# Inputs laid out by the host: x, mem, context and parameters without turns on TensorE

## The reference

```python
def first_block(x, mem, positions, ...):          # per layer
    proj = x @ w_in[l]
    q, k, v, cb, cc, cu, qm, gates = jnp.split(proj, ...)
    q, k = rope(q), rope(k)                        # angles from positions
    y_attn = diff_attention(q, k, v, lam, ...)     # lam from the four lambda vectors
    y_conv = short_gated_conv(cb, cc, cu, conv_w[l])
    y_mem = memory_attention(qm, mem, w_mem_kv[l])
    g = jax.nn.sigmoid(gates)
    merged = g0 * (y_attn @ w_br_attn[l]) + g1 * (y_conv @ w_br_conv[l]) + g2 * (y_mem @ w_br_mem[l])
    x = layer_norm(ALPHA * x + merged @ w_out[l], ln1_g[l], ln1_b[l])
    f = grouped_moe(x, w_router, router_bias, w_exp_gate[l], w_exp_up[l], w_exp_down[l])
    x = layer_norm(ALPHA * x + f, ln2_g[l], ln2_b[l])
```

## Time and profile before

| | us |
|---|---|
| median of 3 runs | 2258.7 |
| lowest and highest | 2258.26, 2258.95 |
| span of the profiled execution | 2261.8 |
| PE busy | 2213.9 (98%) |
| PEld busy | 1399.4 (62%) |
| DVE busy | 1144.6 (51%) |
| ACT busy | 457.5 (20%) |

### The profile page before, as it was taken

The page is one execution under the profiler, slowest core; times in us unless marked ns, Lnnn a source line. Parts: engine busy times, 40 slices in busy tenths (PEclk is TensorE's granted clock), DMA queues, the critical chain, the costliest instruction groups (busy, mean ns, idle before and its releaser), DMA issues.

```text
span 2261.8 us, 24795 instructions
## 1 busy us (share of the span) xinstructions
PE 2213.9 (98%) x9825; PEld 1399.4 (62%) x9825; DVE 1144.6 (51%) x1926; ACT 457.5 (20%) x1046; POOL 3.1 (0%) x20
## 2 busy tenths in 40 slices
PE   8999999999999999999999999999999999999998
PEld 7755444544468765446444486788888888554453
DVE  3755775211137267763111247775556423587666
ACT  2001401211121014122111236420000102352110
POOL 0000000000000000000000000000000000000000
PEclk9999999999999999999999999999999999999999
DMA  8445934799983449435999902003222124403340
GB/s 345 149 178 218 385 141 175 285 399 426 428 358 134 164 155 422 167 149 216 392 425 428 420 33 113 1 1 112 75 75 89 52 103 180 155 10 149 140 177 19
DMA packets 38800, 454.71 MB, mean 201 GB/s; under 512 B 5288, under 2 KB 9242, under 8 KB 11034
## 3 DMA queue, kind: packets, MB, share of 16 engines
q1 hardware_dynamic: 35520, 449.85, 49.2%
q10 hardware_dynamic: 3162, 3.21, 0.4%
HBM read 452.00 MB, written 1.05 MB: 200 GB/s over the span
## 4 chain that ended last, share of the span: by engine, by line
PE 82%; DMA 8%; DVE 7%; DVEq 2%; issue 1%; ACT 1%; SPq 0%; ACTq 0%
PE banks L603 79%; DMA ring<-in_w_exp_up 7%; PE banks L1726 1%; PE banks L759 1%; DVE ring L3040 1%; DVE tiny L3250 1%; DVE tiny L2589 1%; DVE arena L2603 0%; DVE arena L3265 0%; DVE ring L2334 0%; DVE arena L2308 0%; DMA ring<-in_w_in 0%; DVE banks L2586 0%; DVEq L2309 0%; PE banks L1192 0%
## 5 line engine op out<-in xcount | busy, mean ns | idle before, releaser
L603 PE MATMUL banks<-ring,arena 128*64 128x512 f32 (+2 forms) x3302 | 960.7, 546 | 14.5 <-DMA ring<-in_w_exp_up 4.9
L603 PEld LDWEIGHTS banks<-ring,arena 128*128 128x128 f32 (+1 forms) x3302 | 449.5, 166 | 485.4 <-issue 450.7
L603 PE MATMUL banks<-arena 128*128 128x128 f32 (+7 forms) x1584 | 243.9, 344 | 3.7 <-issue 1.7
L603 PE MATMUL banks<-X,ring 128*128 128x256 f32 x1024 | 224.8, 382 | 0.8 <-DVE arena L2542 0.5
L603 PEld LDWEIGHTS banks<-X,ring 128*128 128x128 f32 x1024 | 195.8, 192 | 29.7 <-issue 2.3
L603 PEld LDWEIGHTS banks<-arena 128*128 128x128 f32 (+2 forms) x1584 | 155.3, 173 | 66.4 <-issue 34.9
L603 PE MATMUL banks<-arena,ring 128*128 128x256 f32 (+1 forms) x736 | 179.1, 399 | 0.1
L603 PEld LDWEIGHTS banks<-arena,ring 128*128 128x128 f32 x736 | 138.7, 190 | 36.8 <-issue 14.4
L2433 DVE TENSOR_TENSOR arena<-arena,banks 128x512 f32<-128x512 f32 x16 | 11.0, 687 | 281.9 <-ACT arena L1874 281.9
L603 PE MATMUL banks<-ring 128*128 128x256 f32 x616 | 137.0, 379 | 0.0
L603 PEld LDWEIGHTS banks<-ring 128*128 128x128 f32 x616 | 117.0, 190 | 16.3 <-issue 0.5
(11 more groups left out here) (369 smaller groups left out, 1923.6 us busy)
## 6 DMA issues: line engine op xcount, KB each, us to landing
ring<-in_w_in SPq DMA_DIRECT2D x38, 2048.0 KB, 11.8
ring<-in_w_exp_up SPq DMA_DIRECT2D x32, 2048.0 KB, 16.2
ring<-in_w_exp_down SPq DMA_DIRECT2D x32, 2048.0 KB, 12.3
ring<-in_w_exp_gate SPq DMA_DIRECT2D x30, 2048.0 KB, 13.5
ring<-in_w_ada SPq DMA_DIRECT2D x24, 2048.0 KB, 10.7
ring<-in_w_ffn SPq DMA_DIRECT2D x22, 2048.0 KB, 7.8
ring<-in_w_out SPq DMA_DIRECT2D x8, 2048.0 KB, 13.4
ring<-in_w_down SPq DMA_DIRECT2D x8, 1408.0 KB, 6.0
```

The source lines that it names most:

```text
L603: ins = nc.tensor.matmul(out, weights, moving, start=start, stop=stop)
```

## The change

- The host lays out x, mem and the context with features on partitions (`x_turned`, `mem_turned`, `ctx_turned`, each [128, 8, 256]), and all parameter vectors as 246 columns of one array (`columns`, [128, 246]).
- All turns of these on TensorE go, with the copies out of PSUM on DVE and ACT.
- SP issues x and the first tile in three pieces each, by feature chunks 0 to 2, 2 to 4 and 4 to 8; the matmuls of the first tile go in the same three pieces.
- SP no longer waits for the parameters ahead of the third tile. DVE, ACT and TensorE each wait for all of them (8 transfers now) where they come to need them: TensorE after the second tile.
- mem, the rows of x (for the residual sum) and the context are issued by SP after `w_br_conv`'s tile.

```diff
-PARAM_DMAS = 23
+PARAM_DMAS = 8
+FIRST_PIECES = ((0, 2), (2, 4), (4, 8))
...
-            for tc in range(TC):
-                sp.dma_start(raw["x"][:, tc, :], a["x"][tc * P:tc * P + P, :]).then_inc(s_x[tc], 16)
...
-                    if l == 0 and i == 2:
-                        sp.dma_start(raw["mem"], a["mem"].rearrange("(c p) d -> p c d", p=P)).then_inc(s_inputs, 16)
-                        sp.wait_ge(s_params, PARAM_DMAS * 16)
                     src = block_of("w_in", l * 16 + c)
                     if l == 0 and i == 0:
-                        sp.dma_start(ring[:, 0, 0:TILE // 2], src[:, 0:TILE // 2]).then_inc(s_half_tile, 16)
-                        sp.dma_start(ring[:, 0, TILE // 2:TILE], src[:, TILE // 2:TILE]).then_inc(s_loaded[0], 16)
+                        for n, (k0, k1) in enumerate(FIRST_PIECES):
+                            landed = s_tile_piece[n] if n < len(s_tile_piece) else s_loaded[0]
+                            sp.dma_start(X[:, k0:k1, 0:T], a["x_turned"][:, k0:k1, :]).then_inc(s_x[n], 16)
+                            sp.dma_start(ring[:, 0, k0 * 512:k1 * 512], src[:, k0 * 512:k1 * 512]).then_inc(landed, 16)
...
                 tile(block_of("w_br_conv", l))
                 if l == 0:
+                    sp.dma_start(memT[:], a["mem_turned"]).then_inc(s_inputs, 16)
+                    sp.dma_start(xres, a["x"].rearrange("(c p) d -> p c d", p=P)).then_inc(s_x_rows, 16)
+                    sp.dma_start(X[:, :, T:2 * T], a["ctx_turned"]).then_inc(s_ctx_loaded, 16)
...
-            pe.wait_ge(s_half_tile, 16)
-            for half in range(2):
-                pe.wait_ge(*x_copied[half])
-                if half:
+            for n, (k0, k1) in enumerate(FIRST_PIECES):
+                pe.wait_ge(s_x[n], 16)
+                if k1 < DC:
+                    pe.wait_ge(s_tile_piece[n], 16)
+                else:
                     next_tile()
                 for c, b in enumerate(FIRST_BANKS):
-                    for k in range(4 * half, 4 * half + 4):
+                    for k in range(k0, k1):
...
             tile_features(X, T, "act")
-            pe.wait_ge(s_inputs, 16)
             pe.wait_ge(s_params, PARAM_DMAS * 16)
-            b = ring_bank("dve")
-            nc.tensor.transpose(bank[b][:, 0:104], stackA[0:104, :], ident[0:104, 0:104])
...
-            turned_input("mem", "act")
...
-                    pe.wait_ge(s_ctx_loaded, 16)
-                    turned_input("ctx_2", "act", lambda k0, k1: filler(1, k0, k1))
-                    filler(1, 6, DC)
+                    filler(1, 0, DC)
...
             act.dma_start(pos_i, a["positions"][0, :].partition_broadcast(P)).then_inc(s_turns, 16)
             act.dma_start(invf[:], a["inv_freq"]).then_inc(s_turns, 16)
+            act.dma_start(vecs[:], a["columns"]).then_inc(s_params, 16)
             for i, n in enumerate(("lambda_q1", "lambda_k1", "lambda_q2", "lambda_k2")):
                 act.dma_start(lamrows[:, i, :, :], a[n].partition_broadcast(P)).then_inc(s_params, 16)
             act.dma_start(sinks[:], a["sink_2"].rearrange("l h -> (l h)").partition_broadcast(P)).then_inc(s_params, 16)
             act.dma_start(wr[:], a["w_router"].rearrange("(k p) n -> p k n", p=P)).then_inc(s_params, 16)
             act.dma_start(rbias[:], a["router_bias"].rearrange("(o n) -> o n", o=1)).then_inc(s_params, 16)
```

More of the change, by code:

```diff
@@ L1062, in _ @@
             pe.wait_ge(s_ones, 1)
[L1064 to L1078, removed]
-                for half in range(2):
-                    transposes([raw["x"][:, tc, (4 * half + c) * P:(4 * half + c) * P + P] for c in range(4)],
-                               ring_bank("dve"), "dve")
-            x_copied = (last[2], last[3])
-            pe.wait_ge(s_half_tile, 16)
-            for half in range(2):
-                pe.wait_ge(*x_copied[half])
-                if half:
+            for n, (k0, k1) in enumerate(FIRST_PIECES):
[3 more added lines that the diff above has]
+                else:
                     next_tile()
                 for c, b in enumerate(FIRST_BANKS):
-                    for k in range(4 * half, 4 * half + 4):
+                    for k in range(k0, k1):
                         ins = mm(bank[b][:, 0:T], slot(0, DC, 512)[:, k, c * P:c * P + P], X[:, k, 0:T],
                                  start=(k == 0), stop=(k == DC - 1))
-                    if half:
+                    if k1 == DC:
                         full(ins, b, "act")
@@ L1756, in _ @@
             fn = nc.scalar.activation
[L1759 to L1767, removed]
-                act.dma_start(st[r0:r0 + n, :], src).then_inc(s_params, 16)
             act.dma_start(pos_i, a["positions"][0, :].partition_broadcast(P)).then_inc(s_turns, 16)
             act.dma_start(invf[:], a["inv_freq"]).then_inc(s_turns, 16)
-            for i, n in enumerate(("q_norm_2", "k_norm_2")):
-                for half in range(2):
-                    act.dma_start(stackC[42 + 2 * i:44 + 2 * i, 64 * half:64 * half + 64], a[n]).then_inc(s_params, 16)
+            act.dma_start(vecs[:], a["columns"]).then_inc(s_params, 16)
             for i, n in enumerate(("lambda_q1", "lambda_k1", "lambda_q2", "lambda_k2")):
@@ L1778, in _ @@
             act.dma_start(rbias[:], a["router_bias"].rearrange("(o n) -> o n", o=1)).then_inc(s_params, 16)
-            assert len(rows) + 4 + 4 + 3 == PARAM_DMAS
+            assert 1 + 4 + 3 == PARAM_DMAS
             def take():
@@ L1901, in _ @@
             act.drain().then_inc(s_gate_copied, 1)
-            def input_turned(dst, t0):
-                for c in range(0, DC, 2):
-                    done(nc.scalar.copy(dst[:, c:c + 2, t0:t0 + T], take()[:].rearrange("p (c t) -> p c t", c=2)))
-            input_turned(memT, 0)
+            act.wait_ge(s_params, PARAM_DMAS * 16)
             act.wait_ge(s_lam, 1)
@@ L1994, in _ @@
                 filler_copied(0)
-                if l == 0:
-                    input_turned(X, T)
-                else:
+                if l:
                     for i in range(2 * 2):
@@ L2444, in _ @@
             drain().then_inc(s_ones, 1)
-            for tc in range(TC):
-                for c in (0, 4):
-                    done(v.tensor_copy(X[:, c:c + 4, tc * P:tc * P + P], take()[:].rearrange("p (c t) -> p c t", c=4)))
             dve.wait_ge(s_turns, 32)
@@ L2476, in _ @@
             drain()
-            b = take()
-            v.tensor_copy(vecA[:], b[:, 0:104])
-            v.tensor_copy(vecB[:], b[:, 128:224])
-            done(v.tensor_copy(vecC[:], b[:, 256:302]))
-            turn[0] += 1
-            drain()
+            dve.wait_ge(s_params, PARAM_DMAS * 16)
             for i in range(2):
@@ L3375, in _down_blocks, with _columns @@
     return np.stack(tiles)
+def _columns(np, inputs):
+    rows = [np.asarray(inputs.pop(n)).reshape(-1, P) for n in ("ln1_g", "ln1_b")]
+    rows += [np.asarray(inputs[n]).reshape(-1, P) for n in ("ln2_g", "ln2_b")]
+    rows += [np.asarray(inputs.pop(n)).reshape(-1, P) for n in ("g_mix_2", "g_ffn_2")]
+    rows.append(np.asarray(inputs["g_final_2"]).reshape(-1, P))
+    rows += [np.asarray(inputs.pop(n)).reshape(-1, P) for n in ("b_ada_2", "conv_w", "diff_subln_g", "c_2", "c_ctx_2")]
+    rows += [np.concatenate([np.asarray(inputs.pop(n))] * 2, axis=1) for n in ("q_norm_2", "k_norm_2")]
+    return np.concatenate(rows, axis=0).T
 def kernel(**inputs):
@@ L3386 @@
     inputs = dict(inputs)
+    for name in ("x", "mem", "ctx_2"):
+        rows = np.asarray(inputs[name]).reshape(T, DC, P)
+        inputs[name.replace("_2", "") + "_turned"] = rows.transpose(2, 1, 0)
+    inputs.pop("mem")
+    inputs["columns"] = _columns(np, inputs)
     inputs["w_ffn_2"] = _gates_and_ups(np, np.asarray(inputs.pop("w_gate_2")), np.asarray(inputs.pop("w_up_2")))
```

25 lines of the change are left out of this document (13 added, 12 removed).

## The result

The changed kernel takes 2285.3 us (median of 4, 2285.16 to 2286.05) against 2258.8 us of the kernel before beside it, a ratio of 1.0118, interval [1.0104, 1.0131]. It is 26.5 us slower. I had forecast 2260.1 us, and 2263.8 us as the upper end. Most of the loss lies at two places far from the edit, which the prediction doesn't mention.

What follows compares the result with a forecast made beforehand. TensorE's own line of work was taken as the bound, busy 98% of the span. Parameters +0.8, clock +2.4 and context -1.75 summed to +1.4 us, 2260.1 us for the timed runs, with 8 in 10 from 2251.0 to 2263.8.

Steps and rivals of the forecast that it cites:

- TensorE goes on at 42.7 us: Ahead of the third tile: the parameter wait of 6.9 us gives back the start's whole gain, +0.8 us.
- the other pieces land at the same rate, 0.42 MB per us: At the start: the later pieces of x and the first tile land by about 12.5 us.
- I take 5.8 us: At the start: time of TensorE's first product, which needs the first pieces of x and the tile, 0.79 MB.
- No wait: In the first tile: the half-speed products need the last piece at about 15 us, after it has landed.
- The clock after the wait: Behind the parameter wait: 6.9 us of idling costs TensorE its full clock, +2.4 us, bounds 0 and 3.4.
- turns don't warm the clock: At the start: turns do not count as clock work, so the first tile still takes 16.2 us without them.
- The context turns: At 407 us: removing four groups of turns between the filler's products saves 0.44 us each, -1.75 us in all.
- What costs nothing: Behind w_br_conv: mem, x rows and context, 3 MB or 7.3 us of transfer, land long before use, 0 us.
- The parameters did not come in time: Rival at the start: parameters in time, 7.9 us saved, 2250.8 us; partial form 2253.6 us; together 0.33.
- Small packets starve: Rival: the table moves only when SP is dry; TensorE resumes at 45.0 us, +4.8, 2263.5 us; 0.13 with longer hold.
- ACT is held in issuing: Rival at the start: ACT's hold in issuing past 22 us delays the second tile's copies; chance 0.03.
- The 6.1 us that the start should have given: At the start: without another hold the third tile begins at 35.8 us, 3.5 from x's turns, 2.6 from parameters and mem.

Runs made afterwards that it cites:

- e1: The changed kernel with 104 semaphore increments on TensorE's queue ahead of its first product; 2266.45 us, ratio 1.0033 to the kernel before.
- e4: The kernel before the change with 152 semaphore increments on TensorE's queue ahead of its first turn, no other edit; 2293.07 us, ratio 1.015.
- g3: The kernel before with only the context part of the change (its turns and copies gone, SP loads it behind w_br_conv); 2271.54 us, ratio 1.0053.
- f2: The changed kernel with 16 tiny float32 products ahead of TensorE's first product, and the router table sent as 128 rows; 2272.48 us, ratio 1.006.
- f3: The changed kernel with 16 tiny float32 products ahead on TensorE, and SP's parameter wait put back ahead of the third tile's load; 2273.48 us.
- f4: The changed kernel with 16 tiny float32 products ahead on TensorE, and ACT issuing the parameters only after the first tile's first piece landed; 2280.30 us.
- g4: g3 with 33 semaphore increments on TensorE ahead of its first turn; 2256.63 us, ratio 0.999 to the kernel before.
- g1: The changed kernel with the router table as 128 rows, and 28 increments and 36 tiny bf16 products as padding on TensorE; 2257.18 us, ratio 0.9992.
- places 71 and 84: Instructions put ahead of the changed kernel's TensorE code: 71 is g3, 2271.54 us; 84 is g1 with 84 instructions of padding, 2257.72 us.
- g2: The changed kernel with the router table as 128 rows and no padding; 2272.56 us, ratio 1.006 to the kernel before.

## Why the prediction was wrong

**The whole: a stall that no step names.** The sum had +0.8 for the parameters, +2.4 for the clock and -1.75 for the context, and put the code of the deleted turns at nothing. Of the 26.5 us, 10.4 are the two stalls of 4.95 and 5.47 us and some 5 the half clock behind them (10.2 us at half). Nothing in the prediction speaks of TensorE's code, though the diff removes 104 of its instructions and the kernel has two branches over 365 or more. Shown by e1 and e4, each way round, and by g3 with a third of the edit. It isn't the only miss: e1, with the code back in its place, still took 2266.45 us, above my upper end, and that is the next term.

**"TensorE goes on at 42.7 us": mis-sized, 49.9 us.** The mechanism is as forecast: equal turns, the table last, SP's queue full until the end. The queues of the changed kernel in 28 to 32 us, 28 packets a microsecond each where I had 27 (packets, MB, share):

```profile
q1 hardware_dynamic: 112, 1.62, 95.8%
q10 hardware_dynamic: 113, 0.01, 1.9%
```

f2 and f3 show it from two sides. The failing input is "the other pieces land at the same rate, 0.42 MB per us". The queues by 14 us, of the changed kernel and then of the kernel before:

```profile
q1 hardware_dynamic: 1297, 2.20, 48.6%
q10 hardware_dynamic: 1020, 0.51, 13.8%
```

```profile
q1 hardware_dynamic: 663, 4.57, 81.8%
q10 hardware_dynamic: 400, 0.16, 4.2%
```

SP's has moved 2.20 MB where the old one had moved 4.57, and ACT's 1020 packets where it had 400. Both queues carried mostly packets of 1 KB and less, and the engines were idle two fifths of the time in 10 to 14 us (DMA share 0.61); why they were, stays open. The missing 2.4 MB are 5.6 us of SP's queue: dry at about 47.5 and not 42.0. The table, which I had let begin at 10 us, sent its first packet of 64 bytes at 12.9 us, had a tenth through at 18.2 and nine tenths at 45.9, 29.6 a microsecond, and sent the last at 49.2. Nor did the rest go in 0.3 us once SP's queue was dry. Term: +8.0 and not +0.8.

**"I take 5.8 us" for the first product: wrong, 8.8 us, and without effect.** The DMA share in 4 to 7 us was 0.70 at 211 GB/s, where the old kernel had 432. f4 shows that the parameters' packets aren't the cause; what is, stays open (SP's own issues took up to 1.6 us each, the x pieces go in rows of 1 KB). e1 shows that it cost nothing, since the parameters came later.

**"No wait" for the other pieces: wrong by 1.5 us**, hidden by the same wait.

**The clock after the wait: right.** +2.6 us for 2.4. That turns don't warm the clock held too, within 0.5 us: the first 64 products, without the waits between, took 30.5 us behind no turns and 30.0 behind 4 us of them.

**The context turns: right.** The landmarks moved by 1.77 us for 1.75; g4 has 2.2 at the medians.

**What costs nothing: right**, no wait for mem, the x rows or the context is among TensorE's waits.

**The rivals.** The parameters did not come in time, so the Trainium skill, "DMA: Bandwidth & Descriptors", section "Queues, rings and completion order", by which the small pieces would have needed few turns, disagrees with the trace: the 64-byte pieces took a turn each, 113 against 112. "Small packets starve" was nearer in time (45.0 us) and wrong in kind: they moved all along. "ACT is held in issuing" happened, 9.97 us, and cost nothing here; in f4, 23.74 us, it cost a wait of 10.2.

By the runs' own sum, the change without the stalls and with the table as rows is worth about nothing at the start and 2 us at the context: g1 at -1.7 and g4 at -2.2 us. The 6.1 us that the start should have given did not come in g1 either: its first pieces are as late (waits of 2.54 and 1.79 us), and the third tile starts at about 40.8 us (20.14 and 48 products of 0.431) for 41.9.

## What to carry to other kernels

When an edit adds or removes instructions on an engine that is the bound, count them, and look behind every taken branch of that engine for a gap put down to "issue"; if there is one, pad or trim until it goes before judging the edit. Here both stalls hung on at most 13 instructions (places 71 and 84). And when a wait that kept two queues apart is removed, count packets and not bytes: a table of 1024 short rows in one queue can take as long as 14 MB in the other (12.9 to 49.2 us).

## What the runs showed of the hardware that I had not expected

- A branch over some 390 instructions on TensorE costs nothing or 4.9 to 5.8 us by where it stands in its block of 256, and in the changed kernel the stalls were followed by 3.4 and 6.8 us of half clock.
- An increment of a semaphore on TensorE's queue took 0.16 us (17.0 us for 104); a bf16 product of four columns 0.03 us (1.10 us for 36); a float32 one 0.44 us (6.99 us for 16).
- With mostly packets of 1 KB and less in two queues the 16 DMA engines moved 371 GB/s in 8 to 10 us, and 159 GB/s in 10 to 14 us, idle two fifths of the time; with one of the queues held, 404 and 436 GB/s (f4), the second with larger packets in it.
- The last of ten issues of ACT, 0.1 KB in size, held ACT for 9.97 us, and for 23.74 us when the issues came later, beside 16 KB packets (f4). Behind the table as 128 rows it took 0.6 us (f2, g1, g2).
